# Softmax factors applied to the value products once per head pair, turns of the weights one unit sooner, and two product tiles moved in the order

## The chip, the cores and the metric

The kernel runs on one core of a Trainium2 chip. The metric is the device time of one execution in microseconds (us), from its own measurement; the median of three runs is taken.

## What is computed

Two transformer stacks in sequence, each of depth 2, on 512 tokens of width 1024 in float32. The change lies in the mixer of the first stack, in its softmax attention, which is run by two kinds of heads:

```python
def blocked_attention(q, k, v, scale):
    ...
    s = jnp.einsum('bqkgd,btkd->bkgqt', qblk, k).astype(jnp.float32) * scale
    p = jax.nn.softmax(s, axis=-1).astype(v.dtype)
    return jnp.einsum('bkgqt,btkd->bqkgd', p, v)

def parallel_mixer(h, w_in, ...):
    proj = h @ w_in
    q_g, k_g, v_g, q_lat, kv_lat = jnp.split(proj, IN_OFFSETS, axis=-1)
    # 8 grouped query heads over 2 key heads, head size 64, with norm and rotary
    o_g = blocked_attention(q_g..., k_g, v_g, GQA_HEAD_DIM ** -0.5)
    c_q = rms_norm(q_lat, mla_q_norm)        # latents, from which 8 more heads come
    c_kv = rms_norm(kv_lat[..., :MLA_KV_RANK], mla_kv_norm)
    o_m = blocked_attention(q_m[:, :, :, None, :], k_m, v_m, MLA_QK_DIM ** -0.5)
    merged = jnp.concatenate([rms_norm(o_g, out_norm_gqa), rms_norm(o_m, out_norm_mla)], axis=-1)
    return merged @ w_o
```

After the mixer come a cross attention over 256 memory tokens and a mixture of experts, then (twice) the second stack's mixer and feed-forward part.

## The kernel before

One Python object (`Order`) writes out a single list of steps for the whole computation. Each engine's program walks this list and issues its own share of each step, in the list's order, with semaphore waits written by hand. So each engine executes strictly in the order of the list, and an instruction that waits holds back everything behind it on its engine. PSUM has eight banks, handed out by `take()` (the one released longest ago) and given back by `drop()`. Work that depends on a result from another engine is put off by one or more `tick()`s with `later.append`.

**Attention** (`Order.attention`, line 321). There are 8 pairs of heads per layer, in the order `SEQ["mix"]` = 4, 0, 1, 2, 3, 5, 6, 7; pairs 0 to 3 are grouped-query heads (keys `kh`, `kl`), pairs 4 to 7 are latent heads (keys `mk`). A pair has 8 units: 2 heads times 4 tiles of 128 queries. So a layer has 64 units, numbered n. For each unit:

- `scores`: TensorE multiplies queries and keys to 128x512 (L1482); VectorE takes the negated row maximum (L2606); ScalarE writes the exponential into `Pr` (two tiles named Pr, two named tmp) and leaves the row sum in `st` (L1872).
- `total` and `share`, VectorE, two units later: the reciprocal of the row sum, 128x1 (L2396), and the multiplication of the 128x512 weights by it (L2374). In VectorE's list they stand as: total(n-2), maximum(n), share(n-2).
- `turn_p`, three units later: TensorE turns the four 128x128 blocks (L1490), and one engine copies them into `PT`: VectorE for n % 4 == 1 (`DVE_TURN`, L2624), ScalarE for the other three.
- `values`: per pair four steps kt, each with both heads, 64 columns each (L1532). With `LAG` = 5 the first comes at unit 8i+12 for pair position i, the others two units apart. TensorE waits there for all four turned tiles of a head.
- `att_out`: ScalarE copies the pair's 128x512 output to `oT`; GpSimd squares it (L2171) and adds squares up (L2176, `osq_add`). For pair 7 ScalarE makes the square from PSUM. `osum` (TensorE, L1546) sums the squares over features three ticks later (for pair 7, inside the output product); then `oscale`, GpSimd's power, a turn (L1419) and `y`.

**Latents in the mixer's head** (`Order.mixer`, line 396). Product tiles of 128 columns are made by `fm` (8 steps of three matmuls, L1346 to L1348), followed by VectorE's `rs` (scaling by the row factor). A statistic goes: `stat` (TensorE, L1405), VectorE L2376, GpSimd power L2123, and at the next tick `turned` (TensorE, L1419) and its use, `lat` (VectorE and ScalarE). The order around them is: tile c0, c1, the `krope` tile, ckv, tick (stat cq), `krope` (three VectorE operations), tick (turned cq, lat cq, stat ck), tile k, tick (turned ck, lat ck), tile q0, and so on.

**Memory keys** (`Order.memory`, line 516): tiles key(0), key(1); `nstat`; key(2); `nturn` (L1335, waits for GpSimd's power of the row statistic); key(3).

Of the kernel before, what the change touches and what calls it, by code (L numbers as in the profile page):

```python
# [7 lines left out]
ALU = mybir.AluOpType  # L8
ACT = mybir.ActivationFunctionType
# [4 lines left out]
NT = 4  # L14
D = 1024
NSTAGE = 6
NW = 3
LAG = 5
NS = 39
# [68 lines left out]
ROUTE = (37, 75)  # L88
DVE_TURN = 1
EARLY = {0: ("k", 0), 1: ("k", 0), 2: ("q0", 0), 3: ("q0", 0), 4: ("q0", 1), 5: ("q0", 1), 6: ("k", 1), 7: ("k", 1)}  # L90
# [14 lines left out]
class Order:  # L105
# [214 lines left out]

    def attention(self, kind, l, npair, nhead, nk, step, between):
        KT = nk // 128
        per = nhead * NT
        nu = npair * per
        ub = {}

        def scores(u):
            b = self.take()
            self.do("scores", kind, l, u, b)
            self.drop(b)  # L330

# [64 lines left out]
    def mixer(self, l):  # L396
# [29 lines left out]
        proj("ckv")  # L426
        self.tick()
        lat("ck", ("ckv",))
        self.do("krope", l, u, i)
# [86 lines left out]
    def memory(self, l):  # L516
# [10 lines left out]
        key(1)  # L527
        self.scale(ns, lambda: key(2))
        key(3)

# [712 lines left out]
def pe_program(eng, S, M, steps):  # L1243
# [25 lines left out]
    for name, *a in steps:  # L1269
# [214 lines left out]
        elif name == "turn_p":  # L1484
            kind, l, n, u = a
            o = claim(u)
            Pr = M.Pr[kind][n % 4]
            q.wait_ge(*S.dve.at("share", kind, l, n))
            for kt in range(NKEY[kind] // 128):
# [21 lines left out]
        elif name == "values":  # L1511
# [11 lines left out]
            for h in range(nh):  # L1523
                g = POS[kind][p] * nh + h
                if kind == "mix":
                    q.wait_ge(*S.act.at("PT", kind, l, NT * g + 3))
                    q.wait_ge(*S.dve.at("PT", kind, l, NT * g + DVE_TURN))
# [213 lines left out]
def act_program(eng, S, M, steps):  # L1741
# [5 lines left out]
    for name, *a in steps:  # L1747
# [114 lines left out]
        elif name == "scores":  # L1862
            kind, l, n, u = a
            i, r = divmod(n, NHEAD[kind] * NT)
            c = 64 + 4 * (n % 8)
# [6 lines left out]
            copy(M.Pr[kind][n % 4][:, :], M.ps[u[0]][:, 0:nk], ("exp", kind, l, n), ("free",) + u, f=ACT.Exp,  # L1872
                 bias=M.st[:, c:c + 1], accum_out=M.st[:, c + 2:c + 3])
        elif name == "turn_p":
            kind, l, n, u = a
            g, qt, KT = n // NT, n % NT, NKEY[kind] // 128
            PT = M.PT[kind]
            if n % 4 == DVE_TURN:
                continue
# [28 lines left out]
        elif name == "att_out":  # L1908
            kind, l, p, u = a
            q.wait_ge(*S.pe.at("values", kind, l, p))  # L1910
            if kind == "mem":
                q.wait_ge(*S.pe.at("point", "memory", l))
                copy(M.moh[:, p, :], M.ps[u[0]][:, :], ("hi", ("mo", l), p))
                continue
            if p in (4, 0):
                q.wait_ge(*S.dve.at("heads", l, "k"))
                q.wait_ge(*S.dve.at("heads", l, "q0"))
            if p != 7:
                copy(M.oT[:, POS["mix"][p], :], M.ps[u[0]][:, :], ("oT", l, p), ("free",) + u)
                continue  # L1920
            copy(M.oT[:, POS["mix"][p], :], M.ps[u[0]][:, :], ("oT", l, p))
            q.wait_ge(*S.pool.at("osq_add", l, OSQ_PAST[p]))
            copy(M.osq[OSQ[p]][:, :], M.ps[u[0]][:, :], ("osq", l, p), ("free",) + u,
                 f=ACT.Square)
        elif name == "orow":
# [187 lines left out]
def pool_program(eng, S, M, steps):  # L2113
# [21 lines left out]
    for name, *a in steps:  # L2135
# [27 lines left out]
        elif name == "att_out":  # L2163
            kind, l, p, u = a
            if kind == "mem" or p == 7:
                continue
            q.wait_ge(*S.act.at("oT", l, p))
            q.wait_ge(*S.dve.at("heads", l, ("q1", "q2")[OSQ[p] // 2]))
# [194 lines left out]
def dve_program(eng, S, M, steps):  # L2363
# [22 lines left out]

    def share(kind, l, n):
        c = 64 + 4 * (n % 8)
        q.wait_ge(*S.dve.at("rc", kind, l, n))
        P = M.Pr[kind][n % 4][:, :]  # L2390
        ts(P, P, M.st[:, c + 3:c + 4], ALU.mult, ("share", kind, l, n))

    def total(kind, l, n):
        c = 64 + 4 * (n % 8)
        q.wait_ge(*S.act.at("exp", kind, l, n))
        ve.reciprocal(M.st[:, c + 3:c + 4], M.st[:, c + 2:c + 3]).then_inc(*S.dve.mark(("rc", kind, l, n)))  # L2396

    def mshare(l, d):
# [10 lines left out]
    for name, *a in steps:  # L2409
# [188 lines left out]
        elif name == "scores":  # L2598
            kind, l, n, u = a
            c = 64 + 4 * (n % 8)  # L2600
            if n > 1:
                total(kind, l, n - 2)
            q.wait_ge(*S.pe.at("scores", kind, l, n))
            if n > 7:
                q.wait_ge(*S.dve.at("share", kind, l, n - 8))
            ve.tensor_reduce(M.st[:, c:c + 1], M.ps[u[0]][:, 0:NKEY[kind]], AX.X, ALU.max, negate=True).then_inc(  # L2606
                *S.dve.mark(("ng", kind, l, n)))
            if n > 1:
                share(kind, l, n - 2)
        elif name == "turn_p":  # L2610
            kind, l, n, u = a
            if n % 4 != DVE_TURN:
                continue
# [21 lines left out]
        elif name == "mshare":  # L2635
            mshare(*a)
        elif name == "share":
            total(*a)
            share(*a)
        elif name == "att_out":  # L2640
            kind, l, p, u = a
            if kind == "mem":
                q.wait_ge(*S.act.at("hi", ("mo", l), p))
                tt(M.mol[:, p, :], M.ps[u[0]][:, :], f(M.moh[:, p, :]), ALU.subtract, ("lo", ("mo", l), p), ("free",) + u)
        elif name == "y":
# [18 lines left out]
            q.wait_ge(*S.act.at("oT", l, i))  # L2664
            keys = [("y", l, g, j)]
# [467 lines left out]
```

## Time and profile before

| what | us |
|---|---|
| runs | 2342.7, 2345.5, 2346.4; median 2345.5 |
| profiled execution, its own time | 2345.05 |
| span of the profiled execution, first to last instruction | 2343.2 |
| TensorE (PE) busy | 2280.9 (97%) |
| VectorE (DVE) busy | 1360.2 (58%) |
| ScalarE (ACT) busy | 893.6 (38%) |
| GpSimd (POOL) busy | 230.8 (10%) |
| granted TensorE clock, mean | 0.995 of full |

The first layer's attention runs from 107.3 to about 230.6 us of the span, the second's from 702 to about 826 us. A busy interval of TensorE contains its pipeline's length, so the pace is read from the distance between starts. The same holds in small for VectorE: the next instruction starts some 0.08 us before the one ahead of it has ended.

### The profile page before, as it was taken

The numbers are of one execution on the slowest core, as the hardware profiler recorded it, in microseconds if no ns is written. First come the engines' busy times: TensorE is split into PE (matmuls) and PEld (weight loads), VectorE is DVE, ScalarE is ACT, GpSimd is POOL, SyncE is SP. The second block draws the span as 40 slices with busy tenths as digits, with TensorE's granted clock in tenths as the row PEclk, the third lists the DMA queues.
The fourth block names the chain that finished last, engine by engine and source line by source line (L and its number), as shares of the span: only waits on it lengthen the run. The fifth ranks groups of instructions, "written<-read, shape, count | busy, mean of one in ns | idle before, by whom it ended". The sixth has DMA issues, their size and how long they took to land.

```text
span 2343.2 us, 28475 instructions
## 1 busy us (share of the span) xinstructions
PE 2280.9 (97%) x10844; PEld 1621.2 (69%) x10844; DVE 1360.2 (58%) x2231; ACT 893.6 (38%) x1550; POOL 230.8 (10%) x190
## 2 busy tenths in 40 slices
PE   8999999999999999999999999999999999999998
PEld 6754876344575478744457788888888778888886
DVE  5696654323659755433347757777435665877722
ACT  4485542111437645211133234444223233444421
POOL 2202201000230220100000011000001002000000
PEclk9999999999999999999999999999999999999999
DMA  4300439999530024899973322333333322333331
GB/s 173 99 6 23 140 149 379 410 410 410 218 101 13 19 90 180 333 409 410 410 302 124 86 90 91 99 96 94 99 99 135 112 77 90 99 99 97 101 96 49
DMA packets 112087, 381.63 MB, mean 163 GB/s; under 512 B 16464, under 2 KB 17232, under 8 KB 111696
## 3 DMA queue, kind: packets, MB, share of 16 engines
q1 hardware_dynamic: 108208, 366.80, 44.0%
q0 software_dynamic: 2304, 8.39, 0.9%
q10 hardware_dynamic: 1440, 4.62, 0.5%
q8 instruction: 87, 1.43, 0.3%
q14 instruction: 48, 0.39, 0.0%
HBM read 363.51 MB, written 6.29 MB: 158 GB/s over the span
## 4 chain that ended last, share of the span: by engine, by line
PE 86%; DVE 6%; DMA 3%; ACT 2%; POOL 1%; issue 1%; SPq 0%; POOLq 0%; DVEq 0%; ACTq 0%
PE ps L1346 11%; PE ps L1347 11%; PE ps L1348 11%; PE ps L1643 8%; PE ps L1370 5%; PE ps L1372 5%; PE ps L1371 5%; PE ps L1665 5%; PE ps L1532 3%; PE ps L1391 3%; PE ps L1389 3%; PE ps L1390 3%; PE ps L1482 2%; PE ps L1490 2%; DMA wa<-in_wu 1%; PE ps L1675 1%
## 5 line engine op out<-in xcount | busy, mean ns | idle before, releaser
L2463 DVE TENSOR_TENSOR wlo<-stage,whi 128x1024 fp32r<-128x1024 f32 x262 | 329.4, 1261 | 294.2 <-ACT whi L1782 293.7
L1346 PE MATMUL ps<-hTh,whi 128*128 128x512 f32 x1120 | 442.6, 395 | 0.0
L1348 PE MATMUL ps<-hTh,wlo 128*128 128x512 f32 x1120 | 437.8, 391 | 0.0
L1347 PE MATMUL ps<-hTl,whi 128*128 128x512 f32 x1120 | 437.7, 391 | 0.0
L1782 ACT ACTIVATE whi<-stage 128x1024 fp32r<-128x1024 f32 x262 | 276.0, 1057 | 328.9 <-PE ps L1372 120.6
L1346 PEld LDWEIGHTS ps<-hTh,whi 128*128 128x128 f32 x1120 | 211.2, 189 | 48.2 <-issue 4.7
L1348 PEld LDWEIGHTS ps<-hTh,wlo 128*128 128x128 f32 x1120 | 211.2, 189 | 44.6
L1347 PEld LDWEIGHTS ps<-hTl,whi 128*128 128x128 f32 x1120 | 211.2, 189 | 42.4
L2367 DVE TENSOR_TENSOR ps<-ps,Rs 128x512 f32<-128x512 f32 x124 | 86.1, 699 | 138.9 <-PE ps L1348 124.9
L2370 DVE SCALAR_TENSOR_TENSOR t<-ps,vecs,t 128x511 f32<-128x511 f32 (+1 forms) x176 | 131.1, 745 | 3.7 <-ACT t L1745 0.7
L2367 DVE TENSOR_TENSOR x<-x,ps 128x512 f32<-128x512 f32 x184 | 116.5, 682 | 28.4 <-PE ps L1372 18.0
L2123 POOL TENSOR_TENSOR st<-st,c 128x4 f32<-128x4 f32 (+2 forms) x47 | 66.0, 1405 | 497.0 <-DVE st L2376 489.5
L1643 PE MATMUL ps<-wa,xin 128*64 128x512 f32 x400 | 94.1, 596 | 3.3 <-DMA wa<-in_wu 1.9
L2606 DVE TENSOR_REDUCE st<-ps 128x1 f32<-128x512 f32 x128 | 86.5, 677 | 18.4 <-PE ps L1482 16.5
L2370 DVE SCALAR_TENSOR_TENSOR th<-th,ps 128x512 f32<-128x512 f32 x16 | 11.0, 688 | 144.5 <-ACT th L1745 144.5
L2148 POOL TENSOR_TENSOR nacc<-nacc,nsq 128x512 f32<-128x512 f32 x52 | 76.3, 1467 | 136.7 <-ACT nsq L1745 131.5
L1745 ACT ACTIVATE inh<-t 128x512 fp32r<-128x512 f32 x44 | 27.8, 633 | 123.7 <-DVE t L2370 123.7
L2370 DVE SCALAR_TENSOR_TENSOR Yl<-ps,st,Yh 128x512 fp32r<-128x512 f32 x32 | 22.7, 747 | 84.3 <-ACT Yh L1745 84.3
L1389 PE MATMUL ps<-whi,inh 128*128 128x512 f32 x176 | 68.9, 391 | 0.0
L1745 ACT ACTIVATE t<-ps,vecs 128x512 f32<-128x512 f32 x88 | 66.9, 763 | 5.0 <-DVE ps L2367 5.0
L2148 POOL TENSOR_TENSOR nacc<-nsq,nsq 128x512 f32<-128x512 f32 x9 | 12.6, 1405 | 570.0 <-ACT nsq L1745 570.0
L1391 PE MATMUL ps<-whi,inl 128*128 128x512 f32 x176 | 68.6, 390 | 0.0
(379 smaller groups left out, 4315.9 us busy)
## 6 DMA issues: line engine op xcount, KB each, us to landing
stage<-in_wpk SPq DMA_DIRECT2D x268, 512.0 KB, 3.6
wa<-in_wd SPq DMA_DIRECT2D x56, 512.0 KB, 15.3
wa<-in_wu SPq DMA_DIRECT2D x54, 512.0 KB, 15.1
wa<-in_wg SPq DMA_DIRECT2D x46, 512.0 KB, 15.4
ws<-in_wg SPq DMA_DIRECT2D x26, 512.0 KB, 13.4
ws<-in_wu SPq DMA_DIRECT2D x24, 512.0 KB, 11.9
wr<-in_wg SPq DMA_DIRECT2D x24, 512.0 KB, 15.3
stage<-in_wd SPq DMA_DIRECT2D x22, 512.0 KB, 16.4
```

The lines of the kernel that those rows point to most:

```text
L1346: pe.matmul(o, h, ah, start=k == 0, stop=False)
L1347: pe.matmul(o, h, al, start=False, stop=False)
L1348: t = pe.matmul(o, lo, ah, start=False, stop=k == 7)
L1370: pe.matmul(o, h, ah, start=c == 0 and kk == 0, stop=False)
L1371: pe.matmul(o, lo, ah, start=False, stop=False)
L1389: pe.matmul(o, ah, h, start=c == 0 and kk == 0, stop=False)
L1391: t = pe.matmul(o, al, h, start=False, stop=last and kk == 1)
L1643: t = pe.matmul(M.ps[u[0]][r, :], M.xin[:, k, r], w[e][:, kk * 512:(kk + 1) * 512], start=k == 0, stop=k == 7)
L1782: ac.activation(M.whi[i % NW][:, :], M.stage[i % NSTAGE][:, :], ACT.Copy).then_inc(*S.whi.mark(("w", i)))
L2367: ve.tensor_tensor(o, a, b, op).then_inc(*S.dve.mark(*keys))
L2370: ve.scalar_tensor_tensor(out=o, in0=a, scalar=s, in1=b, op0=op0, op1=op1).then_inc(*S.dve.mark(*keys))
L2463: ve.tensor_tensor(M.wlo[i % NW][:, :], M.stage[i % NSTAGE][:, :], f(M.whi[i % NW][:, :]), ALU.subtract).then_inc(*S.wlo.mark(("w", i)))
```

## The change

1. VectorE's reciprocal and multiplication per unit (`total`, `share`) are gone. ScalarE's exponential is turned unnormalised, one unit sooner (`turn_p(i - 2)`), and `turn_p` waits for the exponential.
2. A new step `sums`, once a pair, at unit 8i+9: VectorE takes the reciprocal of the pair's eight row sums, each spread over 64 columns, so one instruction with a 128x512 output into `tmp` 4 or 5.
3. A new step `shares`: TensorE turns that tile (four 128x128 blocks) into a bank after the pair's last value product; ScalarE copies the raw output into `oT`, and VectorE multiplies `oT` by the bank. For pair 7 ScalarE's square is made from `oT` after that.
4. `LAG` is 4: a pair's value products start one unit sooner.
5. `DVE_TURN` is (1, 3): VectorE copies two of four turned tiles, ScalarE the other two.
6. In the mixer's head, tile k is made directly after stat cq, ahead of `krope`, turned cq and stat ck.
7. In the memory part, key(2) and key(3) both stand between `nstat` and `nturn`.

```diff
-LAG = 5
+LAG = 4
-DVE_TURN = 1
+DVE_TURN = (1, 3)
...
             if kt == KT - 1:
-                self.do("att_out", kind, l, p, ub[p])
+                b = self.take()
+                self.do("shares", l, p, b)
+                self.do("att_out", kind, l, p, ub[p], b)
                 self.drop(ub[p])
-                if kind == "mix":
-                    self.att_sums(l, p)
+                self.drop(b)
+                self.att_sums(l, p)
...
-            elif i - 2 < nu:
-                self.do("share", kind, l, i - 2)
+            if i > per and i % per == 1:
+                self.do("sums", l, i // per - 1)
             self.tick()
             for p, kt in plan.get(i, []):
                 values(p, kt)
-            if 0 <= i - 3 < nu:
-                turn_p(i - 3)
+            if 0 <= i - 2 < nu:
+                turn_p(i - 2)
...
         self.tick()
+        ready.append(self.fm(s, ns))
         lat("ck", ("ckv",))
...
-        self.scale(ns, lambda: key(2))
-        key(3)
+        def keys():
+            key(2)
+            key(3)
+        self.scale(ns, keys)
...
-            q.wait_ge(*S.dve.at("share", kind, l, n))
+            q.wait_ge(*S.act.at("exp", kind, l, n))
...
+        elif name == "shares":
+            l, p, u = a
+            o = claim(u)
+            q.wait_ge(*S.dve.at("sums", l, POS["mix"][p]))
+            r = M.tmp[4 + POS["mix"][p] % 2]
+            for m in range(NT):
+                t = pe.transpose(o[:, m * 128:(m + 1) * 128], r[:, m * 128:(m + 1) * 128], M.ident)
+            t.then_inc(*S.pe.mark(("shares", l, p)))
...
-            if n > 1:
-                total(kind, l, n - 2)
             q.wait_ge(*S.pe.at("scores", kind, l, n))
...
-            if n > 1:
-                share(kind, l, n - 2)
...
+        elif name == "sums":
+            l, i = a
+            q.wait_ge(*S.act.at("exp", "mix", l, 8 * i + 7))
+            if i > 1:
+                q.wait_ge(*S.pe.at("shares", l, SEQ["mix"][i - 2]))
+            c = 65 + 16 * (i % 2)
+            s = M.st[:, c:c + 15:2].rearrange("p (h m) -> p m h", h=2)
+            ve.reciprocal(M.tmp[4 + i % 2][:, :].rearrange("p (m h f) -> p m h f", m=NT, h=2),
+                          s.unsqueeze(3).to_broadcast([128, NT, 2, 64])).then_inc(*S.dve.mark(("sums", l, i)))
         elif name == "att_out":
-            kind, l, p, u = a
+            kind, l, p, u, *b = a
+            if kind == "mix":
+                q.wait_ge(*S.act.at("oU", l, p))
+                q.wait_ge(*S.pe.at("shares", l, p))
+                o = M.oT[:, POS["mix"][p], :]
+                tt(o, o, M.ps[b[0][0]][:, :], ALU.mult, ("oT", l, p), ("free",) + b[0])
```

## Rows read from the trace of the kernel before

**Rows 1.** The page, part 1: busy us, share of the span, instructions.

```profile
PE 2280.9 (97%) x10844; PEld 1621.2 (69%) x10844; DVE 1360.2 (58%) x2231; ACT 893.6 (38%) x1550; POOL 230.8 (10%) x190
```

**Rows 2.** Busy time by stretch: length, engines (instructions), granted clock, DMA share, GB/s.

```profile
44.70:53.10 8.40, 8.40 (x36) 6.94 (x37) 5.02 (x8) 2.84 (x4) 1.01 (x1) 0.80 0.10 23
...
107.30:121.30 14.00, 11.23 (x44) 5.65 (x44) 13.00 (x30) 9.30 (x22) 0.00 (x0) 1.00 0.20 44
121.30:220.30 99.00, 93.81 (x445) 46.36 (x444) 85.04 (x196) 73.25 (x175) 18.47 (x15) 1.00 0.05 14
```

**Rows 3.** Timeline of PE, grouped-query units: start, length, engine, line, operation.

```profile
142.20 1.08 PE L1532 MATMUL ps<-PT,vg 128*64 128x512 f32 x4
143.21 0.66 PE L1490 MATMUL ps<-c,tmp 128*128 128x128 f32 x4
...
148.19 1.08 PE L1532 MATMUL ps<-PT,vg 128*64 128x512 f32 x4
```

**Rows 4.** Timeline of PE, latent units of the second layer.

```profile
781.90 1.08 PE L1532 MATMUL ps<-PT,vg 128*64 128x512 f32 x4
782.91 0.66 PE L1490 MATMUL ps<-c,Pr 128*128 128x128 f32 x4
...
785.66 1.08 PE L1532 MATMUL ps<-PT,vg 128*64 128x512 f32 x4
```

**Rows 5.** Groups of instructions on DVE: shapes, count | busy us, mean ns | idle before.

```profile
L2374 DVE TENSOR_SCALAR Pr<-Pr,st 128x512 f32<-128x512 f32 x64 | 34.4, 537 | 0.0
L2396 DVE RECIPROCAL st<-st 128x1 f32<-128x1 f32 x128 | 19.9, 155 | 0.6
L2624 DVE COPY PT<-ps 128x512 f32<-128x512 f32 x32 | 21.9, 685 | 6.2 <-PE ps L1490 5.9
```

**Rows 6.** Groups on DVE by form: longer reciprocals, a spread copy, an operation with PSUM.

```profile
L2401 DVE RECIPROCAL st<-st 128x2 f32<-128x2 f32 x16 | 2.6, 162 | 3.7 <-ACT mP L1745 3.5
L2702 DVE RECIPROCAL st<-st 128x4 f32<-128x4 f32 x2 | 0.4, 178 | 0.1
L2531 DVE COPY tmp<-st 128x512 f32<-128x512 f32 x10 | 4.2, 421 | 0.0
L2367 DVE TENSOR_TENSOR mol<-ps,moh 128x512 fp32r<-128x512 f32 x8 | 5.5, 690 | 11.7 <-ACT moh L1745 11.7
```

**Rows 7.** Timeline of all engines at the end of the first layer's attention.

```profile
220.26 0.69 DVE L2606 TENSOR_REDUCE st<-ps 128x1 f32<-128x512 f32 x1 [1.30 <-PE ps L1482]
220.98 0.69 ACT L1745 ACTIVATE tmp<-ps,st 128x512 f32<-128x512 f32 x1 [0.99 <-DVE st L2606]
...
221.57 0.19 ACT L1745 ACTIVATION_READ_ACCUMULATOR tmp<-ps,st 128x1 f32 x1
225.56 1.26 POOL L2176 TENSOR_TENSOR raw<-raw,raw 128x512 f32<-128x512 f32 x1
227.86 2.79 PE L1532 MATMUL ps<-PT,vm 128*64 128x512 f32 x12
```

**Rows 8.** Timeline of all engines around the latent statistics, first layer.

```profile
43.53 0.70 DVE L2367 TENSOR_TENSOR tmp<-ps,mcs 32x512 f32<-32x512 f32 x1
...
44.65 0.65 PE L1419 MATMUL ps<-c,st 128*128 128x128 f32 x4 [1.35 <-POOL st L2123]
45.14 0.95 PE L1405 MATMUL ps<-c,sq 128*128 128x1 f32 x8
45.70 0.75 DVE L2370 SCALAR_TENSOR_TENSOR tmp<-raw,vecs,ps 128x512 f32<-128x512 f32 x1
49.80 0.15 DVE L2376 TENSOR_SCALAR st<-ps 128x4 f32<-128x4 f32 x1
50.03 1.01 POOL L2123 TENSOR_TENSOR st<-st,c 128x4 f32<-128x4 f32 x1 [5.44 <-DVE st L2376]
53.11 0.60 PE L1419 MATMUL ps<-c,st 128*128 128x128 f32 x4
```

**Rows 9.** Timeline, memory part of the first layer: the turn after the row statistic.

```profile
288.34 0.62 PE L1335 MATMUL ps<-c,st 128*128 128x128 f32 x4 [0.61 <-POOL st L2123]
```

More of the change, by code:

```diff
@@ L1525, in pe_program @@
                 if kind == "mix":
-                    q.wait_ge(*S.act.at("PT", kind, l, NT * g + 3))
-                    q.wait_ge(*S.dve.at("PT", kind, l, NT * g + DVE_TURN))
+                    q.wait_ge(*S.act.at("PT", kind, l, NT * g + 2))
+                    q.wait_ge(*S.dve.at("PT", kind, l, NT * g + 3))
                 else:
@@ L1864, in act_program @@
             i, r = divmod(n, NHEAD[kind] * NT)
-            c = 64 + 4 * (n % 8)
+            c = 64 + 2 * (n % 16)
+            if n > 15:
+                q.wait_ge(*S.dve.at("sums", l, n // 8 - 2))
             q.wait_ge(*S.dve.at("ng", kind, l, n))
@@ L1872, in act_program @@
             copy(M.Pr[kind][n % 4][:, :], M.ps[u[0]][:, 0:nk], ("exp", kind, l, n), ("free",) + u, f=ACT.Exp,
-                 bias=M.st[:, c:c + 1], accum_out=M.st[:, c + 2:c + 3])
+                 bias=M.st[:, c:c + 1], accum_out=M.st[:, c + 1:c + 2])
         elif name == "turn_p":
@@ L1877, in act_program @@
             PT = M.PT[kind]
-            if n % 4 == DVE_TURN:
+            if n % 4 in DVE_TURN:
                 continue
@@ L1908, in act_program @@
         elif name == "att_out":
-            kind, l, p, u = a
-            q.wait_ge(*S.pe.at("values", kind, l, p))
+            kind, l, p, u, *_ = a
             if kind == "mem":
+                q.wait_ge(*S.pe.at("values", kind, l, p))
                 q.wait_ge(*S.pe.at("point", "memory", l))
@@ L1914, in act_program @@
                 continue
+            q.wait_ge(*S.pe.at("values", kind, l, p))
             if p in (4, 0):
@@ L1917, in act_program @@
                 q.wait_ge(*S.dve.at("heads", l, "q0"))
[L1918 to L1924, printed above, removed]
+            copy(M.oT[:, POS["mix"][p], :], M.ps[u[0]][:, :], ("oU", l, p), ("free",) + u)
+            if p == 7:
+                q.wait_ge(*S.dve.at("oT", l, p))
+                q.wait_ge(*S.pool.at("osq_add", l, OSQ_PAST[p]))
+                copy(M.osq[OSQ[p]][:, :], M.oT[:, POS["mix"][p], :], ("osq", l, p), f=ACT.Square)
         elif name == "orow":
@@ L2163, in pool_program @@
         elif name == "att_out":
-            kind, l, p, u = a
+            kind, l, p, u, *_ = a
             if kind == "mem" or p == 7:
                 continue
-            q.wait_ge(*S.act.at("oT", l, p))
+            q.wait_ge(*S.dve.at("oT", l, p))
             q.wait_ge(*S.dve.at("heads", l, ("q1", "q2")[OSQ[p] // 2]))
@@ L2385, in signed_sines @@
         after_own()
[L2387 to L2396, printed above, removed]
     def mshare(l, d):
@@ L2599, in dve_program @@
             kind, l, n, u = a
-            c = 64 + 4 * (n % 8)
-            if n > 1:
-                total(kind, l, n - 2)
+            c = 64 + 2 * (n % 16)
             q.wait_ge(*S.pe.at("scores", kind, l, n))
-            if n > 7:
-                q.wait_ge(*S.dve.at("share", kind, l, n - 8))
+            if n > 15:
+                q.wait_ge(*S.act.at("exp", kind, l, n - 16))
             ve.tensor_reduce(M.st[:, c:c + 1], M.ps[u[0]][:, 0:NKEY[kind]], AX.X, ALU.max, negate=True).then_inc(
                 *S.dve.mark(("ng", kind, l, n)))
-            if n > 1:
-                share(kind, l, n - 2)
         elif name == "turn_p":
             kind, l, n, u = a
-            if n % 4 != DVE_TURN:
+            if n % 4 not in DVE_TURN:
                 continue
@@ L2636, in dve_program @@
             mshare(*a)
-        elif name == "share":
-            total(*a)
-            share(*a)
-        elif name == "att_out":
-            kind, l, p, u = a
+        elif name == "sums":
[7 more added lines that the diff above has]
+                          s.unsqueeze(3).to_broadcast([128, NT, 2, 64])).then_inc(*S.dve.mark(("sums", l, i)))
+        elif name == "att_out":
+            kind, l, p, u, *b = a
[4 more added lines that the diff above has]
+                tt(o, o, M.ps[b[0][0]][:, :], ALU.mult, ("oT", l, p), ("free",) + b[0])
             if kind == "mem":
@@ L2663, in dve_program @@
                 q.wait_ge(*(S.dve if g else S.pool).at("lo", ("y", l), i - 2))
-            q.wait_ge(*S.act.at("oT", l, i))
+            q.wait_ge(*S.dve.at("oT", l, i))
             keys = [("y", l, g, j)]
```

## The prediction

> **What bounds the kernel now.** I read the page's busy times first: TensorE is busy for 97% of the span, and no other engine above 58% [rows 1]. So a gain must take TensorE's own work or its waits, and a loss need only add to them. Then the busy times by stretch, because 58% of VectorE is a mean: in the first layer's attention VectorE is busy for 13.0 of 14.0 us in the opening and for 85.0 of the next 99.0, while TensorE is busy for 11.2 and 93.8 [rows 2]. In these 99 us lie the starts of units 8 to 63. The second layer repeats the pattern to 0.1 us, so I work out one layer and double it.
>
> The timelines of TensorE give its pace where nothing waits. From one value step to the second next, four units on, there are 148.19 - 142.20 = 5.99 us with grouped-query scores; from one to the next, two units on, 785.66 - 781.90 = 3.76 with latent scores. The value step itself takes 143.21 - 142.20 = 1.01 of it [rows 3, 4]. A unit thus costs 1.50 or 1.88 us, a pair of 8 units 12.0 or 15.0. Units 8 to 63 are 32 grouped-query and 23 latent ones: 32 x 1.50 + 23 x 1.88 = 91.2; one sum of squares and one turn of factors add some 1.3. Without waits the stretch would take 92.5; it takes 99.0. **Only 6.5 us a layer can be won there.**
>
> **What leaves and enters VectorE.** Per layer 64 scalings of 0.537 us and 64 reciprocals of 0.155 leave: 34.4 + 9.9 = 44.3 us (the rows group 64 scalings of each kind of tile over both layers, the other kind costs about the same) [rows 5]. What enters: 16 more copies of turned tiles at 0.685, 11.0 us [rows 5]; 8 products of `oT` with a bank, by the row of the same shape 0.690, 5.5 us [rows 6]; and 8 reciprocals with 128x512 outputs. Here is the number on which all hangs, and the trace has no such instruction. Its short ones take 0.155 us for one element per partition, 0.162 for two, 0.178 for four [rows 5, 6]: (178 - 155) / 3 = 7.7 ns for each further element. Drawn out, 155 + 511 x 7.7 ns = **4.07 us**. The bounds: below, the copy of the same spread shape, 0.42 us [rows 6], if the slope of the short ones is chance; from the single readings of slope, 7 ns (one to two) and 8 ns (two to four), 3.7 to 4.3, and as these differences are smaller than the scatter of one such instruction (its minimum and maximum are 20 ns apart) I allow 3.5 to 5.2. I take 4.07, since three sizes lie on one line. Then 8 x 4.07 = 32.6 enters, and VectorE's sum is 49.1 in against 44.3 out: it does not get emptier, and its work comes in pieces of 4 us.
>
> By the Trainium skill ("VectorE: DVE Perf Modes", section "First, the fixed hardware budget") the reciprocal is an iterative divide with a repeat count of 8; at the 0.96 GHz that the page's specifications state, that would be an estimate of 512 x 8 / 0.96 = 4.3 us. It agrees with the slope of the rows, and the sum by it would be some 3 us higher.
>
> **What a 4 us piece costs TensorE.** `sums` stands at unit i = 8k+9, behind the maximum of unit i, and ahead of the product for the pair before, the copy of turned tile i-2 and all later maxima. Count from the end of scores(i), with VectorE's instructions 0.08 us closer than their lengths: maximum to 0.65, reciprocal to 4.64, product to 5.25, copy of tile i-2 done at 5.95, its waiter starts at 6.0. That waiter is the second head's first value product of the new pair, two units on, for it needs all four turned tiles. Ahead of it TensorE has: value step 1.01, shares 0.49, three things of the next units (two turns, two scores: 3.00 - 1.01 = 1.99, or 2.75 latent), and the first head's half step 0.45: 3.9 us, or 4.7 latent. **TensorE waits 2.1 us (three times) and 1.3 us (three times).** At i = 9 there is no older pair: no product (5.4 instead of 6.0), no value step, no shares: 5.4 - 2.5 = 2.9 us. Together 6.3 + 3.9 + 2.9 = 13.1 us. After each, the maxima behind are caught up within two units, as VectorE's other work is 0.6 to 1.2 us a unit against 1.5 to 1.9 of TensorE.
>
> Rest of this stretch: `shares` is four turns; four turns take 45.14 - 44.65 = 0.49 us [rows 8]; seven of them 3.4. The sum of squares of pair 3 follows three ticks after its product, which now ends at 5.25 and is followed by two GpSimd operations of about 1.2 each [rows 7], so TensorE waits about 1.0 more there. Of the 6.5 us of old waits I let 5.0 vanish, since a unit's chain to its turn is now maximum and exponential alone, and ScalarE loses a copy in four; 1.5 stay (power of the output's statistic, half tiles of weights). Sum: 13.1 + 3.4 + 1.0 - 5.0 = **+12.5**.
>
> **The opening** (to unit 8) I leave at zero, -1 to +1: VectorE loses work, but the chain maximum, exponential, high part, low part, copy (0.69 + 0.69 + 0.62 + 0.61 + 0.60 per two units) is as long as the 3.0 to 3.5 us that two units take there.
>
> **The tail.** From the last maximum's start at 220.26 to the end of the last value product at 227.86 + 2.79 = 230.65 there are 10.4 us [rows 7]. Afterwards: the row sum is read at 1.5 (221.76 - 220.26), reciprocal to 5.5, product of pair 6 to 6.1, then its squares on GpSimd (2.4 with gaps) to 8.6, the sum of squares 1.0 to 9.6, three value steps 2.8: 12.4. That is +2.0; shares of pair 7 add 0.5, and its square, now behind a copy and a product, comes some 0.3 late for TensorE. **+2.8.** The attention thus costs +15.3 a layer.
>
> **Tile k moved.** Now TensorE waits 1.35 us for GpSimd's power before turned cq, and in the 8.4 us behind it the granted clock is 0.80 on average, so part of it lies at the lower level, 1.2 GHz; at 2.4 GHz throughout it would be 0.2 x 8.4 = 1.7 us shorter, of which I count 1.5 [rows 2, 8]. With tile k ahead the first wait has cover. But tile k was also the only cover between stat ck and turned ck (45.14 and 53.11), and the statistic's VectorE part comes after lat cq [rows 8]. After: tile k runs from 43.30 to 48.85; VectorE then has its scaling 0.65 and, queued behind this, the three `krope` operations, 1.9 (they fill the wait of VectorE today, 43.53 to 45.70), then lat cq and the statistic, 4.25 (45.70 to 49.95), then the power, 1.1: 56.75. TensorE is done with turned cq and stat ck at 50.15 and **waits 6.6 us**. It reaches turned ck 3.7 us later than now. The low clock stretch I keep at 1.5 us, moved to tile q0: an idle of 1.35 is followed by it today, one of 6.6 will be too. So +5.2 a layer; bounds 3.7 (clock stays up) and 6.7 (it stays low twice as long).
>
> **Memory keys.** key(3) covers the 0.61 us wait before the turn [rows 9]: -0.6 a layer, -0.6 to 0. The other moves (LAG, DVE_TURN, waits on other semaphores) are in the sums above; no DMA is moved.
>
> **Sum.** 2 x (15.3 + 5.2 - 0.6) = +39.8 us. Against the profiled execution's own 2345.05 us, which is 0.45 below the median of the runs, that gives 2384.9, rounded **2385 us**. With the reciprocal at 3.5 or 5.2 us, sixteen times, it is 2376 or 2403; with the clock's and the old waits' bounds some 5 more on either side.
>
> **Rivals.**
> - *Plain pace* (not slower). The reciprocal takes 0.4 to 0.7 us. For it: only 7 to 23 ns of difference stand behind the slope. Then no wait arises at `sums`: 3.4 - 5.0 = -1.6 in the stretch, and about -1 in the tail, 2 x -2.6 = -5; with +5.2 and -0.6 a layer +4: 2349. The Trainium skill's general form for VectorE (same page, "The TRN2 errata", 58 cycles and one per element) would give 0.59 us, this case. The rows speak against it.
> - *Plain pace and no new wait at turned ck* (faster). If VectorE's chain behind tile k were hidden, both the 1.35 and the 1.5 of low clock are gained: -5 - 2 x 2.85 - 1 = -12: 2333.
> - *The pieces are absorbed.* The reciprocal is long, but TensorE loses only half of the 13.1 and 2.0 (the old waits at VectorE's queue show a hold being partly hidden). 2385 - 2 x 7.5 = 2370, inside the range.
> - *The clock falls in attention* (slower still). Sixteen waits of 1.3 to 3 us, each followed by a slow stretch of 1.5: +24, 2409. Against it: in the opening now TensorE idles 2.8 of 14.0 us at a granted 1.00 [rows 2].
>
> **How the numbers follow.** Forecast 0.66, absorbed 0.12, clock 0.08, plain pace 0.09, plain pace and faster 0.05. A change of 0.2%, 4.7 us, is about what the measurement tells from none. Slower: 0.66 + 0.12 + 0.08 and a third of plain pace, 0.89; same 0.06; faster 0.05. The range reaches from absorbed with a short reciprocal, 2364, to the long reciprocal, 2404; it leaves the two plain cases and most of the clock's out.
>
> **What would show it.** A group of 16 reciprocals 128x512 at about 4.1 us each; VectorE's busy sum up by about 10 us, not down by 60; TensorE's longest waits at value products, for the turned copy; turned ck waiting 6 to 7 us for GpSimd; stretches of 8 units 14.5 us long with grouped-query scores. If the reciprocal is under 1 us, the forecast falls as a whole.

## The result, with the profile after

The changed kernel takes **2386.35 us** (median of 4 runs, 2384.60 to 2389.76) against 2345.66 us of the kernel before on the same chip (4 runs): a ratio of 1.018, 95% interval [1.016, 1.020]. It is 40.7 us slower; 2385 was forecast. The profiled execution is the slowest of the four, 2389.76 us with a span of 2387.9, so its rows exaggerate by some 3 us.

The page of the changed kernel, part 1, which answers to [rows 1]:

```profile
PE 2311.4 (97%) x10908; PEld 1635.2 (68%) x10908; DVE 1374.4 (58%) x2039; ACT 878.3 (37%) x1518; POOL 231.0 (10%) x190
```

VectorE has 192 instructions fewer and is busy 14.2 us longer. Its groups that came or grew, changed kernel (shapes, count | busy, mean ns | idle before, releaser):

```profile
L2644 DVE RECIPROCAL tmp<-st 128x512 f32<-128x512 f32 x16 | 53.5, 3346 | 0.2
L2624 DVE COPY PT<-ps 128x512 f32<-128x512 f32 x64 | 43.7, 683 | 17.8 <-PE ps L1496 17.4
L2382 DVE TENSOR_TENSOR oT<-oT,ps 128x512 f32<-128x512 f32 x16 | 10.2, 635 | 19.3 <-ACT oT L1759 9.7 <-PE ps L1547 9.7
```

Sixteen reciprocals of 3.35 us are 53.5 us. With 32 more copies (21.8) and the products (10.2), 85.5 us of instructions came in, against 34.4 and 33.0 us of scalings and 19.9 us of reciprocals that left, 87.3 us [rows 5, and the group of the other kind of tile]. So the lengths of VectorE's instructions did not grow. The busy time counts the overlap of neighbours once, and with 192 instructions fewer there is less of it: 192 x 0.08 us are 15 us, an estimate that fits the 14.2. The work is as much as before, but in longer pieces. The waits of TensorE in the changed kernel (total us, times, longest) show who pays:

```profile
PE ps L1538 <- DVE PT L2624: 16.6, 12, 2.1
PE ps L1425 <- POOL st L2138: 14.2, 2, 7.1
```

The first is the value product for a turned tile that VectorE copies late, the second the turned factors of the keys. The first was not among the waits of before; the second was there with at most 1.4 us at a time. One place of each kind, first the mixer's opening, in the timeline of the changed kernel (start, length, engine, line, operation, idle before):

```profile
49.29 0.60 PE L1425 MATMUL ps<-c,st 128*128 128x128 f32 x4
49.49 0.70 DVE L2382 TENSOR_TENSOR ps<-ps,Rx 128x512 f32<-128x512 f32 x1 [4.30 <-PE ps L1354]
50.22 0.69 DVE L2382 TENSOR_TENSOR tmp<-ps,mcs 32x512 f32<-32x512 f32 x1
...
56.48 0.15 DVE L2391 TENSOR_SCALAR st<-ps 128x4 f32<-128x4 f32 x1
56.72 1.01 POOL L2138 TENSOR_TENSOR st<-st,c 128x4 f32<-128x4 f32 x1 [10.65 <-DVE st L2391]
57.78 1.11 PE L1425 MATMUL ps<-c,st 128*128 128x128 f32 x4 [7.10 <-POOL st L2138]
```

TensorE turns the factors of cq at 49.29, without the wait of [rows 8], and takes the sums of squares of ck (stat ck). From there it has nothing to do while VectorE works through tile k's scaling, `krope` and lat cq, and only then reaches the statistic of ck. Turned ck starts at 57.78, where it stood at 53.11. The stretches around it, changed kernel (columns as in [rows 2]):

```profile
49.30:57.80 8.50, 1.40 (x14) 1.31 (x12) 5.63 (x9) 2.86 (x5) 1.01 (x1) 0.70 0.00 0
57.80:68.00 10.20, 10.20 (x41) 8.51 (x42) 3.53 (x5) 2.52 (x4) 0.65 (x1) 0.75 0.19 53
248.60:254.00 5.40, 5.40 (x14) 1.32 (x14) 0.00 (x0) 0.00 (x0) 0.00 (x0) 0.50 0.00 0
```

TensorE works for 1.4 of the first 8.5 us. When it is busy again the granted clock is 0.75 on average over 10.2 us: part of them passes at 1.2 GHz, at a cost of 0.25 x 10.2 = 2.5 us. The third row belongs to the end of the attention, below.

Second, the attention's first value product and the end of the first layer's attention, changed kernel:

```profile
130.41 3.35 DVE L2644 RECIPROCAL tmp<-st 128x512 f32<-128x512 f32 x1
133.68 0.63 DVE L2624 COPY PT<-ps 128x512 f32<-128x512 f32 x1
134.46 1.04 PE L1538 MATMUL ps<-PT,vm 128*64 128x512 f32 x2 [1.68 <-DVE PT L2624]
...
238.37 0.69 DVE L2608 TENSOR_REDUCE st<-ps 128x1 f32<-128x512 f32 x1 [0.61 <-PE ps L1488]
240.57 3.34 DVE L2644 RECIPROCAL tmp<-st 128x512 f32<-128x512 f32 x1
244.38 0.68 DVE L2624 COPY PT<-ps 128x512 f32<-128x512 f32 x1
245.20 1.04 PE L1538 MATMUL ps<-PT,vm 128*64 128x512 f32 x2 [1.80 <-DVE PT L2624]
248.61 5.39 PE L1538 MATMUL ps<-PT,vm 128*64 128x512 f32 x12
```

The copy of a turned tile starts when the reciprocal has ended (in the second place after the product of `oT` too), and the value product waits for it. The last three value steps take 5.39 us; the same twelve matmuls took 2.79 [rows 7]. The granted clock was 0.50 all through them, the lower level (the row of 248.60 to 254.00 above).

### The profile page after: what moved, and what is told of

Its sections match the earlier page's. It is cut to its first block, busy times and chain, and to the rows that moved or that the text cites. A ratio compares the mean times of both kernels' runs of the same rounds, so it can differ in the third digit from the quotient of the medians.

```text
span 2387.9 us, 28309 instructions
## 1 busy us (share of the span) xinstructions
PE 2311.4 (97%) x10908; PEld 1635.2 (68%) x10908; DVE 1374.4 (58%) x2039; ACT 878.3 (37%) x1518; POOL 231.0 (10%) x190
## 4 chain that ended last, share of the span: by engine, by line
PE 85%; DVE 7%; ACT 3%; DMA 2%; issue 2%; POOL 1%; SPq 0%; POOLq 0%; DVEq 0%; ACTq 0%
PE ps L1352 11%; PE ps L1353 11%; PE ps L1354 11%; PE ps L1657 9%; PE ps L1376 4%; PE ps L1378 4%; PE ps L1377 4%; PE ps L1679 4%; PE ps L1395 3%; PE ps L1396 3%; PE ps L1397 3%; PE ps L1538 3%; PE ps L1488 2%; PE ps L1496 2%; DMA wa<-in_wu 1%
## 5 line engine op out<-in xcount | busy, mean ns | idle before, releaser
L1488 PE MATMUL ps<-mk,mq 128*128 128x512 f32 x128 | 67.0, 611 | 3.0 <-ACT vm L1759 3.0
```

The source lines that it names most:

```text
L1488: t = pe.matmul(o, x[:, qt * 128:(qt + 1) * 128], k, start=i == 0, stop=i == len(terms) - 1)
```

## The experiments

Theory: the time is lost in two places that have nothing to do with each other, the length of one VectorE instruction and the order in the mixer's opening; the design itself is worth about nothing, because TensorE had only 6.5 us a layer to win.

**The reciprocal on eight numbers (e1_small).** The changed kernel with the division in two steps:

```
-            ve.reciprocal(M.tmp[4 + i % 2][:, :].rearrange("p (m h f) -> p m h f", m=NT, h=2),
-                          s.unsqueeze(3).to_broadcast([128, NT, 2, 64])).then_inc(...)
+            r = M.st[:, 224:232]
+            ve.reciprocal(r.rearrange("p (m h) -> p m h", h=2), s).then_inc(*S.dve.mark())
+            after_own()
+            ve.tensor_copy(M.tmp[4 + i % 2][:, :].rearrange("p (a f) -> p a f", a=8),
+                           r.unsqueeze(2).to_broadcast([128, 8, 64])).then_inc(...)
```

> The changed kernel, but the reciprocal is taken of the eight row sums alone (128x8) and then spread to 128x512 by a copy like the one that took 0.42 us before; everything else stays. Theory (the 3.35 us piece on VectorE holds the copy of turned tile i-2 and with it the value products): the waits of TensorE at the value products for the turned copy go, the attention falls from 139.9 us a layer to about 121 (123.3 before the change), the time to 2352 (2349 to 2357). Rival (the new design as a whole is the cost: unnormalised turns, shares on TensorE, product of oT): the attention stays above 132 us and the time above 2370.

Measured: 2357.43 us, ratio 1.005 [1.004, 1.007]: 28.9 us of the 40.7 are gone. The rival, that the design as a whole is the cost (a time above 2370, an attention above 132 us), is refuted: the attention of the first layer is 123.7 us long. That is more than the 121 expected, and 5 us less came back; the time is 0.4 us outside the theory's range. Its groups:

```profile
L2645 DVE RECIPROCAL st<-st 128x8 f32<-128x8 f32 x16 | 3.2, 198 | 0.2
L2647 DVE COPY tmp<-st 128x512 f32<-128x512 f32 x16 | 6.8, 427 | 0.6
L2382 DVE TENSOR_TENSOR oT<-oT,ps 128x512 f32<-128x512 f32 x16 | 11.0, 688 | 28.0 <-ACT oT L1759 18.8 <-PE ps L1496 9.1
```

The pair of instructions takes 0.6 us instead of 3.35. The last row names what is new: in front of the product VectorE now idles 28.0 us, most of it for ScalarE's copy into `oT`.

**Tile k back in its place (e2_nomix).** The changed kernel without its sixth part:

```
         self.tick()
-        ready.append(self.fm(s, ns))
         lat("ck", ("ckv",))
```

> The changed kernel with tile k back in its old place, between stat ck and turned ck. Theory (the 7.1 us wait at turned ck and the low clock behind it are the price of the move, the old 1.35 us wait and its low clock come back): 6 to 7 us a layer less, 2373 (2370 to 2376). Rival (the wait only collects slack that later waits would have had anyway): within 3 us of 2386.

Measured: 2370.56 us, ratio 1.011 [1.010, 1.013], 15.8 us less than the changed kernel; the profile's attention starts at 107.98 instead of 114.44. The rival (within 3 us of the changed kernel) is refuted. TensorE's wait is the old one:

```profile
PE ps L1424 <- POOL st L2137: 2.7, 2, 1.4
```

**Both (e3_both).** The two edits together.

> Both: small reciprocal with a spread copy, and tile k in its old place. If the two causes are all of the loss and independent, the time is that of the kernel before less the old waits that the lighter VectorE saves (2.6 us a layer) and the memory keys (0.6 a layer): 2339 (2335 to 2343). If there is a third cost in the design, it lies above 2346.

Measured: 2347.10 us (11 runs), ratio 1.001 [1.000, 1.002]. Not faster, and above the 2346 that had been set for a third cost, though only by 1 us. From e1_small to e3_both the tile is worth 10.3 us, what the prediction had given it (10.4). Timeline of this kernel, a grouped-query pair:

```profile
137.78 0.59 ACT L1758 ACTIVATE oT<-ps 128x512 f32<-128x512 f32 x1
138.39 0.69 DVE L2381 TENSOR_TENSOR oT<-oT,ps 128x512 f32<-128x512 f32 x1 [1.52 <-PE ps L1495]
138.78 2.03 PE L1537 MATMUL ps<-PT,vg 128*64 128x512 f32 x4
139.00 0.68 DVE L2623 COPY PT<-ps 128x512 f32<-128x512 f32 x1
```

VectorE takes its list in order. The product stands ahead of the copy of turned tile i-2 and waits until ScalarE, busy with exponentials and copies, has made `oT` (137.78 + 0.59 = 138.37; the row names a turn as the releaser of its 1.52 us, but the product starts at 138.39, when `oT` is there). The tile stays uncopied, though its turn had long ended, and the value step takes 2.03 us instead of 1.08.

**The reciprocal in four pieces (e4_split)** of 128x128, one every second unit (and all four for the last pair):

```
-            if i > per and i % per == 1:
-                self.do("sums", l, i // per - 1)
+            if kind == "mix" and per < i < nu and i % 2:
+                self.do("sums", l, i // per - 1, (i % per // 2,))
+            elif kind == "mix" and i == nu + 1:
+                self.do("sums", l, i // per - 1, (0, 1, 2, 3))
```

> The changed kernel with the same 128x512 of reciprocals a pair, cut into four of 128x128 at units 8k+9, 11, 13, 15 (for the last pair all four at unit 65, as now). VectorE's work is the same to 0.3 us a pair. Theory (it is the length of the piece that counts, as TensorE has 3 to 4 us of other work before the copy is needed): a piece of about 0.9 us is covered, and the time falls by 15 to 25 us, to about 2366. Rival (VectorE's sum counts, being full in this stretch): it stays within 5 us of 2386.

Measured: 2372.08 us, ratio 1.012 [1.010, 1.013]: 14.3 us less than the changed kernel, 6 more than the theory had. Its group of reciprocals, and then TensorE's wait for the turned copy:

```profile
L2647 DVE RECIPROCAL tmp<-st 128x128 f32<-128x128 f32 x64 | 59.6, 940 | 0.3
```

```profile
PE ps L1540 <- DVE PT L2626: 7.3, 8, 1.8
```

VectorE's reciprocals are even longer in sum than in the changed kernel (59.6 against 53.5 us; its busy time is the same, 1372.8 against 1374.4), and yet a third of the loss is gone and the wait falls from 16.6 to 7.3 us. The place to read it is where the pieces are spread. From the first maximum of an attention to its last, the changed kernel takes 122.2 us in both layers, this one 114.6 and 114.9, and e1_small 110.9: spreading gives 7.5 of the 11.3 us that the short reciprocal gives. (1.7 us of the changed kernel's stretch is a low clock, see below, which the other two don't have there.) So it is the **length of the piece** in front of a copy that hurts there, more than the sum. In the tail the four pieces still come together, 3.76 us, and two of the eight waits, 1.8 us each, lie there. Over the whole kernel 14.7 us remain to e1_small. Length and position in the list were changed together and are not told apart.

**The product behind the copy (e5_defer).** e3_both, with the steps behind `shares` put off to the end of the unit:

```
-                self.do("att_out", kind, l, p, ub[p], b)
-                ...
-                self.att_sums(l, p)
+                pend.append((p, b))
...
             if 0 <= i - 2 < nu:
                 turn_p(i - 2)
+            finish()
```

> The two-step division (reciprocal of 128x8, spread copy) with tile k in its old place, as in e3_both, and now the copy of the product (att_out), VectorE's multiplication and the row sums of a pair come behind the turned copy of unit i-2 in the same unit, so that this copy no longer stands behind a multiplication that waits for ScalarE. Theory (third cost): in e3 the value step behind each multiplication took 2.03 us instead of 1.08, so 0.95 us for each of about 7 pairs a layer, 13 us in two layers, at least 8 of which come back: 2337 us (2333 to 2341), faster than before. Rival: TensorE is full in the 8-unit stretches and the waits that the design removes were never there; then it stays at 2344 us or above.

Measured: 2344.08 us (11 runs), ratio 0.9994 [0.9985, 1.0003]. Timeline of this kernel, the same pair:

```profile
137.50 0.69 DVE L2631 COPY PT<-ps 128x512 f32<-128x512 f32 x1 [0.65 <-PE ps L1503]
138.37 0.69 DVE L2389 TENSOR_TENSOR oT<-oT,ps 128x512 f32<-128x512 f32 x1 [0.18 <-ACT oT L1766]
138.75 1.08 PE L1545 MATMUL ps<-PT,vg 128*64 128x512 f32 x4
```

The mechanism is shown: the value step is back at 1.08 us. The size was wrong, 3.0 us and not 13. I had priced 0.95 us for every pair; in the profiles the two attentions became 4.4 us shorter in all (first layer 121.8 instead of 123.7). Up to the last maximum they gained 2.8 and 3.5 us, as only some of the pairs had lost by it. Each tail gave back 1.0: with the product put off, the last sum of squares waits 1.9 us for GpSimd where it waited 0.7. The theory's 2337 is refuted, and the rival's bound (2344 or above) is just met: with these costs removed, the design is worth 0.06%, which can't be told from nothing.

**The same in the changed kernel (e10_defer_long)**, long reciprocal and moved tile k kept.

> The changed kernel, reciprocal over 128x512 and moved tile k and all, with the copy of the product and its multiplication put behind the turned copy of unit i-2, as in e5. Theory: with the long reciprocal the turned copy comes late behind that, and the multiplication is hidden: within 3 us of the changed kernel's 2386. Rival: the multiplication's wait adds to the reciprocal: at least 4 us less, as the step from e3 to e5 gave 3.

Measured: 2382.89 us, ratio 1.016 [1.014, 1.018], 3.5 us less than the changed kernel, between the theory's 3 and the rival's 4. The intervals of the two kernels overlap, so the time decides nothing, and the trace has to. The wait for the turned copy fell from 16.6 to 10.5 us:

```profile
PE ps L1546 <- DVE PT L2632: 10.5, 12, 1.7
```

The product's own 0.6 us had stood between the reciprocal and the copy: 6.1 us less over twelve waits are 0.5 us each. Against this stand longer waits for GpSimd: ahead of the sums of squares 3.8 us where there were 1.5, and 1.2 us that are new, so 2.6 of the 6.1 are left.

**The mixer's opening in a chain (e6_pipe).** e5_defer, and in the whole opening each product tile is made one step sooner (tile k behind `krope`).

```
-        lat("ck", ("ckv",))
         self.do("krope", l, u, i)
         self.drop(u)
+        ready.append(self.fm(s, ns))
+        lat("ck", ("ckv",))
         self.tick()
...
         def head_tile(tile):
             proj(tile)
+            ready.append(self.fm(s, ns))
             self.tick()
...
```

> e5_defer, and in the mixer's opening every product tile is made one step ahead of where it was (tile k behind the three operations of krope, each later tile one turn earlier), so that one tile's matmuls stand between the statistics and each turn of factors. Theory: the waits at turned cq (1.35 us a layer) and turned ck are covered and the low-clock stretch behind them (1.5 us a layer) goes: 5 to 6 us below e5, about 2331 us. Rival: the wait only moves to the next turn, since ScalarE's and GpSimd's copies set the pace of this stretch: within 1 us of e5, or above it.

Measured: 2345.47 us (11 runs), ratio 1.0003 [0.9994, 1.0012]; not told from the kernel before, and within 1.4 us of e5_defer, where the rival stood. Timeline of TensorE in this kernel:

```profile
49.19 0.60 PE L1434 MATMUL ps<-c,st 128*128 128x128 f32 x4
...
55.99 0.60 PE L1434 MATMUL ps<-c,st 128*128 128x128 f32 x4
...
85.72 1.11 PE L1434 MATMUL ps<-c,tmp 128*128 128x128 f32 x4 [2.85 <-DVE tmp L2544]
```

Both statistics' turns start without a wait and at the full clock, and 30 us later a turn waits 2.85 us for VectorE's `tmp`, itself then 1.11 us long where the others take 0.60. Waits for `tmp` are 6.3 us in all here (three times, up to 2.8) and 1.9 (twice, up to 1.0) in e5_defer. The low clock moved with the wait: from 44 to 58 us the granted clock is 1.00 here (0.76 in e5_defer), and from 84 to 92 us it is 0.57 (1.00 in e5_defer). Both stretches cost some 3.4 us (0.24 x 14 and 0.43 x 8). A tile made sooner is cover moved, not cover won.

**`krope` ahead of tile k (e7_krope)**, in the changed kernel:

```
-        ready.append(self.fm(s, ns))
-        lat("ck", ("ckv",))
         self.do("krope", l, u, i)
         self.drop(u)
+        ready.append(self.fm(s, ns))
+        lat("ck", ("ckv",))
         self.tick()
```

> The changed kernel, with the three operations of krope put ahead of tile k's matmuls and row sums, so that VectorE reaches the statistics of the keys sooner. Theory: part of the 7.1 us at the turned factors of the keys is the row sums and copies of tile k that VectorE and GpSimd do ahead of the statistics; the wait falls to about 5.2 us, 2 us a layer, 2382 us. Rival: the wait is the chain of statistics, copy and turn itself, which starts when the latent sums are there; then the time stays within 1 us of the changed kernel's.

Measured: 2382.97 us, ratio 1.016 [1.014, 1.018], 3.4 us less than the changed kernel. The two intervals overlap here too; what is shown is the wait. Timeline of this kernel:

```profile
48.20 0.70 DVE L2382 TENSOR_TENSOR ps<-ps,Rx 128x512 f32<-128x512 f32 x1 [0.28 <-PE ps L1354]
48.81 0.74 DVE L2385 SCALAR_TENSOR_TENSOR tmp<-raw,vecs,ps 128x512 f32<-128x512 f32 x1
52.90 0.15 DVE L2391 TENSOR_SCALAR st<-ps 128x4 f32<-128x4 f32 x1
54.19 1.11 PE L1425 MATMUL ps<-c,st 128*128 128x128 f32 x4 [4.80 <-POOL st L2138]
```

The wait fell from 7.10 to 4.80, 2.3 us a layer: the three operations of `krope` behind tile k's scaling, which the prediction had in its sum with 1.9. The 4.80 that are left are lat cq ahead of the statistic, and no tile beside them.

**The memory's keys (e8_keys, e9_oldkeys).** First the kernel before with the change's seventh part alone:

```
-        self.scale(ns, lambda: key(2))
-        key(3)
+        def keys():
+            key(2)
+            key(3)
+        self.scale(ns, keys)
```

> The kernel before, with the second key turn too put between the statistics and the copy of the factors. Theory: the wait of 0.6 us at the key turn goes in both layers: 1.2 us, 2344 us, within 0.2% of before, and all that this part of the change could bring. Rival: the wait moves to the factors' turn behind it, no change at all.

Measured: 2343.76 us, ratio 0.9993 [0.9984, 1.0002]. In the trace the wait of 0.61 us [rows 9] is gone; the time moved by 1.3 us, where 1.2 were expected, which is below what the interval tells from nothing. Then e5_defer with that part taken back, the same lines in the other direction:

> e5_defer, with the key turns of the memory as in the kernel before (one behind the statistics, the other behind the factors). In e5 the first attention starts 1.8 us later than before, with TensorE at its lower clock from 46.9 to 52.1 us of the span where it was before from 47.0 to 50.3. Theory: that longer low clock comes from how the two key turns lie at the statistics; undone, 1.8 us a layer come back: 2340.5 us (2338 to 2342). Rival: it is chance of the execution or of the program, no matter where the key turns lie: within 1.5 us of e5_defer's 2344.

Measured: 2343.30 us (11 runs), ratio 0.9996 [0.9987, 1.0006], within the rival's bounds. The granted clock of the stretch did not change with it. It could hardly have: the key turns lie at about 288 us [rows 9], long behind the stretch from 44 to 58 us in the first layer, so this run tests the theory weakly. Busy time from 44 to 58 us in e5_defer, in this kernel, and in the kernel before:

```profile
44.00:58.00 14.00, 13.16 (x52) 11.01 (x53) 7.75 (x12) 5.01 (x8) 1.79 (x2) 0.76 0.20 66
```

```profile
44.00:58.00 14.00, 14.00 (x55) 11.61 (x54) 7.56 (x11) 5.38 (x8) 1.01 (x1) 0.76 0.14 39
```

```profile
44.00:58.00 14.00, 13.35 (x60) 11.12 (x61) 8.95 (x13) 5.39 (x8) 1.60 (x2) 0.88 0.18 60
```

0.76, 0.76 and 0.88: 0.12 of 14 us are 1.7 us a layer that neither kernel's code around there explains. The opening's order is the same in all three. Why the clock stays low longer in two of them is open.

## Why the prediction was right, and where its sizes were off

Its sum was +39.8 us, and 40.7 were measured. The cause was right: undoing its two terms brings the kernel back to within 3 us of the time before (2347.10 against 2344.28 on the same chip). That the sum came within 1 us is luck. Its largest price, the reciprocal, was 0.72 us too high, sixteen times, 11.5 us; with the true price the same sum would have given 2373. Terms that it had too low or at nothing made this up: a low clock at two places of the attention, less cover in the latent units, and a longer wait and a longer low clock at tile k. The terms in the profile, one layer, where the measured numbers come from the profiled executions:

| term | predicted | measured |
|---|---|---|
| opening, to unit 8 | 0 | +0.7 (13.95 to 14.66) |
| stretch to the last maximum | +12.5 | +10.3 (99.0 to 109.3) |
| tail | +2.8 | +5.7 |
| start of the attention (tile k) | +5.2 | +7.1 |
| memory keys | -0.6 | about -0.6 |

Twice the measured column is 46.4 us, the two profiled spans are 44.7 apart (2387.9 and 2343.2), and the medians 40.7; the changed kernel's profiled execution was the longest of its four.

- **The reciprocal.** 4.07 us was estimated, 3.35 measured, below the lower bound of 3.5. The step that was off was the third point of the line: 155, 162 and 178 ns [rows 5, 6] were taken as a slope of 7.7 ns. With the sizes of the experiments the slope is (3347 - 940) / 384 = 6.3 and (940 - 198) / 120 = 6.2 ns an element; 149 + 6.25 n gives 155 and 162 and 3349, and 174 where 178 was read from two instructions. (It gives 199 and 949 for 8 and 128 elements, where 198 and 940 were measured.) A slope read from differences of 7 and 16 ns and drawn out over 511 elements was a quarter too steep. The Trainium skill's repeat count of 8 ("VectorE: DVE Perf Modes", section "First, the fixed hardware budget") had given an estimate of 4.3 us; the measurement decides, and it is 3.35. VectorE's busy sum was said to rise by about 10 us and rose by 14.2, but not for the reason given: with the true reciprocals the lengths in and out nearly cancel (85.5 and 87.3 us), and the rise is the missing overlap.
- **The stretch.** The count of what stands ahead of the waiting value product holds for the grouped-query pairs. It is read from starts, since a busy interval contains the pipeline's length (timeline of TensorE, changed kernel):

```profile
131.71 1.07 PE L1538 MATMUL ps<-PT,vm 128*64 128x512 f32 x2
134.46 1.04 PE L1538 MATMUL ps<-PT,vm 128*64 128x512 f32 x2 [1.68 <-DVE PT L2624]
...
146.70 1.07 PE L1538 MATMUL ps<-PT,vg 128*64 128x512 f32 x2
148.67 1.07 PE L1538 MATMUL ps<-PT,vg 128*64 128x512 f32 x2 [0.90 <-DVE PT L2624]
...
191.01 2.13 PE L1538 MATMUL ps<-PT,vg 128*64 128x512 f32 x4
...
225.94 1.07 PE L1538 MATMUL ps<-PT,vm 128*64 128x512 f32 x2
229.10 1.07 PE L1538 MATMUL ps<-PT,vm 128*64 128x512 f32 x2 [2.10 <-DVE PT L2624]
```

  A half value step takes 0.45 us. At the first pair 2.75 us lie between the halves, 2.3 lost, where 2.9 were said and 2.2 follow for a reciprocal 0.72 shorter; at the three grouped-query pairs behind it 1.97, so 1.5 lost, where 2.1 and 1.4. In the latent units it fails: two pairs lose 1.05 (steps of 2.13 instead of 1.08) and the third 3.16 - 0.45 = 2.7, where 1.3 was said and 0.6 follow for the shorter reciprocal. Together 11.6 against 13.1. The 1.0 us for the sum of squares of pair 3 did not come: the changed kernel waits ahead of such sums only twice, 0.7 us in each tail. The sum lacked another term. Behind the third latent pair's wait of 2.10 us TensorE's granted clock falls, in both layers:

```profile
229.10:234.51 5.41, 5.41 (x14) 2.70 (x15) 2.53 (x4) 2.75 (x8) 1.75 (x2) 0.68 0.01 3
```

  0.32 of 5.41 are 1.7 us a layer. Then 11.6 + 3.4 + 1.7 = 16.7 against 10.3 measured leaves 6.4 us for the old waits that vanished, where the prediction let 5.0 go: by difference, nearly all of its 6.5. With a reciprocal of 3.35 us the count would have been 8.1 (seven times 0.72 less), and the latent pairs are 3 us above it. I had counted all of their units' extra length as cover; why less of it covers was not tried. For the third pair the trace shows one reason. VectorE is in arrears there with the scalings of the grouped-query output (timeline of VectorE, changed kernel):

```profile
222.61 1.44 DVE L2385 SCALAR_TENSOR_TENSOR tmp<-oT,vecs,raw 128x512 f32<-128x512 f32 x1
224.58 3.33 DVE L2644 RECIPROCAL tmp<-st 128x512 f32<-128x512 f32 x1
```

  The reciprocal starts 1.4 us before the first half step (225.94); at the pairs before it was 3.5 us (187.53 and 191.01). A grouped-query pair is 14.24 us long (reciprocals at 144.12 and 158.36), where 14.5 was said.
- **The third cost.** The product of `oT`, 0.6 us in VectorE's queue ahead of the copy, was in the sum, and the trace of e10_defer_long shows it. What the sum had not was ScalarE's part: the product must wait for `oT`, 1.52 us in e3_both. Behind the long reciprocal most of this is hidden (19.3 us of idle before the products against 28.0 in e1_small), so it shows little in the changed kernel, and it spoiled the design once the reciprocal was short.
- **The tail.** The order of events was as told, wait and all. But 2.6 of the 5.7 us are the last twelve matmuls at the lower clock (5.39 against 2.79), and 0.7 the sum of squares ahead of them (1.71 against 1.05). The prediction had kept a falling clock for a rival of its own, all over the attention; it came at two places of each layer, here (5.39 at 865.92 too), behind the waits of 1.80 and 0.73 us, and behind the third latent pair.
- **Tile k.** The wait at turned ck was 7.1 instead of 6.6 us, and stat cq was 0.55 late already (42.01 instead of 41.46). The stretch at low clock was counted at 1.5; a quarter of 10.2 us, 2.5, was measured. Forecast 5.2, measured 6.5 against the mixer of e2_nomix (114.44 - 107.98), and 5.2 against that of e3_both, whose own clock stays low longer. The two edits don't add: 28.9 + 15.8 = 44.7 alone, 39.3 together. The clock can explain it: the profile of e2_nomix has the low clock of the attention at one of the four places only (the last twelve matmuls of the first layer), though its waits for the turned copy are the same (16.5 us, 12 times), so its 15.8 hold some of the clock that e1_small gives back too. The medians' share of this is not known.
- **"Only 6.5 us a layer can be won."** This held best. With the reciprocal short, the tile back and the product out of the way, the attention of the first layer is 121.8 us long instead of 123.3, and the kernel takes the same time. A grouped-query pair takes 12.42 us (136.36 to 148.78) against 12.5: what the design saves there, the four turns of `shares` (0.49 us) take.

The rivals: "plain pace" and "faster" fell with the row of 3.35 us; "absorbed" by the 11.6 us of waits, where it had half of 13.1; "the clock falls" is right at two of the eight waits of a layer, 1.7 and 2.6 us, some 9 us in all.

## What to carry to other kernels

An engine that is 58% busy can still set the pace through the length of one instruction: price what stands in line behind it, and put a long operation (the reciprocal here costs by the element that it writes) on the few numbers before they are spread. Moving work to cover one wait uncovers another unless the chain behind it gets shorter. And a saving on VectorE is worth no more than what TensorE waits for it, here 6.5 us a layer, less what the new way adds to TensorE.

## What was not expected of the hardware

- The reciprocal takes 6.25 ns for each element of a partition's output, at 8, 128 and 512 alike, where a copy of 128x512 from the same eight numbers takes 0.427 us in all.
- TensorE's clock at the end of the attention. In the changed kernel the last twelve matmuls ran at 0.50 of full (5.39 us), behind waits of 1.80 and 0.73 us. In the kernel before, the opening of the first layer's attention, where TensorE idles 2.8 of 14 us, has a granted clock of 1.00 [rows 2], but the same opening in the second layer has 0.88 (702.1 to 716.1 us), which the prediction's "second layer repeats the pattern" missed. Over the traces, the last twelve take 4.5 to 5.4 us in nine of ten layers of the kernels with 128x512 or four 128x128 reciprocals, in two of ten with the short one (e6_pipe and e9_oldkeys), and in none of the kernel before and e8_keys. Behind the same wait of 2.1 us at the third latent pair, the changed kernel has 0.68 and e2_nomix 1.00. The kernels e5_defer and e9_oldkeys have the same order there and nearly the same wait ahead of the sum of squares (1.92 and 1.91 us), and in the first layer the twelve take 2.80 us in one and 5.39 in the other (in the second layer 2.80 and 2.79):

```profile
227.80 2.80 PE L1545 MATMUL ps<-PT,vm 128*64 128x512 f32 x12
```

```profile
226.31 5.39 PE L1543 MATMUL ps<-PT,vm 128*64 128x512 f32 x12
```

So the low clock is not fixed by the wait alone, and single terms of some 2 us a layer in these accounts can be the clock's. What decides it was not settled.
